# First two projection units on x without its inverse root, and a second transposition of x

## What is computed

```python
u = rmsnorm(x, norm_w)          # x * rsqrt(mean(x*x) + 1e-6) * norm_w, per token
proj = u @ w_in                 # 2048 x 20528
ml_i, ml_f, dn_b, dn_a = ...    # 48 small gate columns of proj
qkv = silu(causal_conv(proj[:, dn_qkv], width 4))   # 3 x 2048 columns
q, k = l2norm(heads(q)), l2norm(heads(k))
...
```

## Time and profile before

| | |
|---|---|
| time, median of 3 runs | 1907.54 us (1907.08 to 1909.92) |
| profiled execution | 1906.96 us, of which its span is 1905.2 us |
| PE busy | 1885.3 us (99%) |
| DVE busy | 1407.6 us (74%) |
| ACT busy | 911.0 us (48%) |
| DMA | 393.17 MB, 206 GB/s over the span |
| chain that ended last | PE 92%, DVE 4%, POOL 1%, ACT 1% |

### The profile page before, as it was taken

How to read it: one execution, slowest core, us unless ns; L and a number is a source line. 1 busy time by engine, 2 the same in 40 slices (tenths; PEclk the granted TensorE clock), 3 DMA queues, 4 the chain that set the end, 5 groups by cost and what they waited for, 6 DMA issues and landing times.

```text
span 1905.2 us, 27734 instructions
## 1 busy us (share of the span) xinstructions
PE 1885.3 (99%) x10964; PEld 1635.8 (86%) x10964; DVE 1407.6 (74%) x2068; ACT 911.0 (48%) x1394; POOL 328.5 (17%) x550
## 2 busy tenths in 40 slices
PE   8999999999999999999999999999999999999998
PEld 8999999878888989888888888888888888888886
DVE  5786877767989788889989667666464676657675
ACT  6546455445433433434445465554444455544544
POOL 1034425161212222313223100000000000111000
PEclk9999999999999999999999999999999999999999
DMA  8555454546788787777888857655656543544563
GB/s 263 149 159 177 124 176 144 155 155 194 263 271 288 255 270 238 238 261 248 288 293 307 297 188 233 232 177 186 196 169 203 175 133 126 185 147 150 186 224 132
DMA packets 209745, 393.17 MB, mean 206 GB/s; under 512 B 13000, under 2 KB 62448, under 8 KB 208208
## 3 DMA queue, kind: packets, MB, share of 16 engines
q1 hardware_dynamic: 191248, 323.17, 52.0%
q0 software_dynamic: 18224, 68.17, 11.2%
q10 hardware_dynamic: 144, 0.07, 0.0%
HBM read 387.13 MB, written 4.23 MB: 205 GB/s over the span
## 4 chain that ended last, share of the span: by engine, by line
PE 92%; DVE 4%; POOL 1%; ACT 1%; issue 1%; DMA 0%; SPq 0%; DVEq 0%; ACTq 0%; POOLq 0%
PE GB L2188 50%; PE GB L2215 19%; PE GB L2200 9%; PE GB L2203 5%; PE SB L419 1%; PE SB L1759 1%; DVE WL L2112 1%; PE SB L1751 1%; POOL TB L1122 1%; POOL XB L1125 1%; PE SB L1858 1%; PE SB L1865 1%; PE SB L829 1%; PE SB L1216 1%; ACT WH L2107 0%
## 5 line engine op out<-in xcount | busy, mean ns | idle before, releaser
L2112 DVE TENSOR_TENSOR WL<-raw,WH 128x1024 fp32r<-128x1024 f32 x605 | 730.9, 1235 | 180.3 <-ACT WH L2107 179.1
L2107 ACT ACTIVATE WH<-raw 128x1024 fp32r<-128x1024 f32 x605 | 622.7, 1059 | 312.2 <-PE GB L2188 226.2
L2188 PE MATMUL GB<-WH,uHL 128*128 128x512 f32 x1792 | 484.6, 392 | 1.2 <-DVE WL L2112 1.2
L2188 PEld LDWEIGHTS GB<-WH,uHL 128*128 128x128 f32 x1792 | 333.2, 188 | 69.2 <-issue 1.3
L2215 PE MATMUL GB<-uHL,WH 128*128 128x256 f32 x2048 | 291.4, 285 | 1.6 <-DVE uHL L455 1.6
L2188 PE MATMUL GB<-WH,hHL 128*128 128x512 f32 x1024 | 279.4, 395 | 0.0
L2188 PE MATMUL GB<-WL,uHL 128*128 128x512 f32 x896 | 276.1, 389 | 0.0
L2215 PEld LDWEIGHTS GB<-uHL,WH 128*128 128x128 f32 x2048 | 264.0, 192 | 2.9 <-DVE uHL L455 1.8
L2188 PEld LDWEIGHTS GB<-WH,hHL 128*128 128x128 f32 x1024 | 190.6, 188 | 41.1 <-issue 2.7
L1446 DVE SCALAR_TENSOR_TENSOR macc<-wm,csil,macc 128x512 f32<-128x512 f32 x300 | 209.5, 748 | 2.7 <-DMA wm<-in_w_mod 1.5
L2188 PEld LDWEIGHTS GB<-WL,uHL 128*128 128x128 f32 x896 | 168.2, 188 | 35.5
(11 more groups left out here) (408 smaller groups left out, 1911.9 us busy)
## 6 DMA issues: line engine op xcount, KB each, us to landing
raw<-in_w_in SPq DMA_DIRECT2D x512, 512.0 KB, 4.5
raw<-in_w_out SPq DMA_DIRECT2D x96, 512.0 KB, 5.2
wm<-in_w_mod POOLq DMA_DIRECT2D x64, 512.0 KB, 5.5
wm<-in_w_mod POOLq DMA_DIRECT2D x64, 256.0 KB, 4.3
xin<-in_x SPq DMA_DIRECT2D x4, 512.0 KB, 5.8
E<-decay_rows POOLq DMA_DIRECT2D x4, 512.0 KB, 4.2
hres<-in_x POOLq DMA_DIRECT2D x1, 2048.0 KB, 10.7
cin<-in_ctx POOLq DMA_DIRECT2D x1, 2048.0 KB, 11.5
```

Source lines behind the costliest of these rows:

```text
L2107: e.activation(place(s)[0][:, :, :], raw[s % NR][:, :, :], ACT.Copy).then_inc(*wh.inc("WH", s))
L2112: e.tensor_tensor(low[:, :, :], raw[s % NR][:, :, :], f32(high[:, :, :]), sub).then_inc(*wl.inc("WL", s))
L2188: m = e.matmul(banks[j][:, :], x[:, c, 128 * j:128 * j + 128], w[:, k, :], start=i == 0 and k == 0 and n == 0, stop=i == 7 and k == 1 and ...
```

## The change

x is loaded in eight parts of 256 columns, interleaved with the first five weight tiles, and `vcol` is loaded from ACT's queue. PE transposes the unscaled x as it lands; `uH` and `uL` are made from x times `norm_w` alone. Units 0 and 1 (`RAW = 2`) and the gates are computed on them. Slot 0 is computed by `first_pe` in another order (all of `uH` on `WH`, all of `uL` on `WH`, all of `uH` on `WL`). The sums of squares move to slots 2 to 5 and the inverse root to slots 5.5 and 6. The inverse root is spread over a row per token: DVE multiplies the identity by it, PE multiplies `ones` by the result between the two row groups of slot 7 (`norm_pe`), and ACT copies it to `rrow`. DVE multiplies the gates' result by `rrow` (in place of ACT's copy), and the results of units 0 and 1 too (`scaled_dve`, at slots 7 and 15, into `zz`, from which the convolutions then read). ACT scales x in place at slots 8 to 9.5, and x is transposed and split a second time (stage "u2", pairs 0 to 7 at slots 10, 11, 12, 13, 13.5, 14, 14.5 and 15.5), with `uH` of a pair overwritten once the slot of unit 1 that reads it is done. Slot s of unit 2 waits for pair s-16 of the second pass. 8 instead of 30 matmuls of `ones` run at the start.

```diff
+RAW = 2
...
+NXA, NXD, NXP = (2, 3, 4, 5, 6, 7, 8, 8.5, 9, 9.5), (5.5, 6), (6.5,)
...
     steps("u", -1, 2, 100)
     steps("u", 0, 6)
+    at("nxa", 0, NXA)
+    at("nxd", 0, NXD)
+    at("nxp", 0, NXP)
+    at("u2", 0, (10, 11, 12, 13, 13.5, 14, 14.5, 15.5))
     at("gates", 0, GATES)
     steps("cond", 60, 2)
...
-        nx_act = steps("nx_act", "warm", "s0", "s1", "s2", "s3", "sqrt", "x1a", "x1b", "x1c")
-        nx_dve = steps("nx_dve", "ss", "var", "inv", "w2", "wv", "rstd", "x0a", "x0b", "x0c")
+        nx_act = steps("nx_act", "warm", "s0", "s1", "s2", "s3", "sqrt", "row", "x0", "x1", "x2", "x3")
+        nx_dve = steps("nx_dve", "ss", "var", "inv", "w2", "wv", "rstd", "diag")
+        nx_pe = steps("nx_pe", "row")
+        z_dve = steps("z_dve", "z")
...
+        TU, TU2, THB, THA, TCTX, THX, TOA, TOB = 0, 8, 16, 24, 32, 40, 48, 52
...
+        def turn_act(e, base, H, pairs, scale, shift, *free, freed=None):
             for k in range(pairs):
                 if k == 0:
                     for said in free:
                         e.wait_ge(*said)
+                if freed:
+                    e.wait_ge(*freed(k))
...
-            claim(e, bank, 0, g_act.at("c"))
+            claim(e, bank, 0, g_dve.at("c"))
...
-            e.wait_ge(*g_pe.at("g"))
-            e.activation(rw[:, SS, :], SB[0][:, 0:256], ACT.Copy).then_inc(*g_act.inc("c"))
...
-            e.wait_ge(*g_act.at("c"))
+            e.wait_ge(*g_pe.at("g"))
+            e.wait_ge(*nx_act.at("row"))
+            e.tensor_tensor(r(SS), SB[0][:, 0:256], rrow[:, :], mul).then_inc(*g_dve.inc("c"))
+            e.wait_ge(*g_dve.at("c"))
...
         def norm_act(e):
-            e.wait_ge(*init.at("eps"))
-            e.activation(st[:, 62:63], eps[:, 0:1], ACT.Sqrt).then_inc(*nx_act.inc("warm"))
-            for i in range(2):
-                for j in range(2):
-                    n = 2 * i + j
-                    e.wait_ge(x_in[n], 16)
+            for j in range(2):
+                for i in range(2):
+                    n = 2 * j + i
+                    for p in range(4):
+                        e.wait_ge(x_in[4 * j + p], 16)
                     if n >= 2:
                         e.wait_ge(*nx_act.at(f"s{n - 2}"))
-                    e.activation(s_junk[:, 1024 * j:1024 * j + 1024], xin[:, i, 1024 * j:1024 * j + 1024], ACT.Square,
-                                 accum_out=st[:, n:n + 1]).then_inc(*nx_act.inc(f"s{n}"))
+                    e.activation(s_junk[:, 1024 * i:1024 * i + 1024], xin[:, i, 1024 * j:1024 * j + 1024], ACT.Square,
+                                 accum_out=st[:, 2 * i + j:2 * i + j + 1]).then_inc(*nx_act.inc(f"s{n}"))
+                    yield
             e.wait_ge(*nx_dve.at("var"))
             e.activation(st[:, 4:6], rs[:, 0:2], ACT.Sqrt).then_inc(*nx_act.inc("sqrt"))
-
-        XPARTS = {"a": slice(0, 512), "b": slice(512, 1024), "c": slice(1024, 2048)}
-
-        def scaled_act(e, c):
-            e.activation(xin[:, 1, XPARTS[c]], xin[:, 1, XPARTS[c]], ACT.Copy, scale=st[:, 5:6]).then_inc(*nx_act.inc("x1" + c))
-
-        def scaled_dve(e, c):
-            e.tensor_scalar(xin[:, 0, XPARTS[c]], xin[:, 0, XPARTS[c]], st[:, 4:5], None, mul).then_inc(*nx_dve.inc("x0" + c))
-
-        def busy_pe(e):
-
-            for said, n in ((init.at("ones"), 15), ((x_in[2], 16), 5), ((x_in[3], 16), 6), (nx_dve.at("ss"), 4)):
-                e.wait_ge(*said)
-                for _ in range(n):
-                    e.matmul(SB[3][:, 0:128], ones[:, :], ones[:, :], start=True, stop=True, skip_group_check=True)
+            yield
+            e.wait_ge(*nx_pe.at("row"))
+            e.activation(rrow[:, :], SB[2][:, 0:256], ACT.Copy).then_inc(*nx_act.inc("row"))
+            yield
+            e.wait_ge(*tr_pe.at("t", TU + 7))
+            for j in range(2):
+                for i in range(2):
+                    c = slice(1024 * j, 1024 * j + 1024)
+                    e.activation(xin[:, i, c], xin[:, i, c], ACT.Copy, scale=st[:, 4 + i:5 + i]).then_inc(*nx_act.inc(f"x{2 * j + i}"))
+                    yield
 
         def norm_dve(e):
             e.wait_ge(*nx_act.at("s3"))
             e.tensor_tensor(st[:, 4:6], st[:, 0:4:2], st[:, 1:4:2], add).then_inc(*nx_dve.inc("ss"))
             e.wait_ge(*nx_dve.at("ss"))
             e.tensor_scalar(rs[:, 0:2], st[:, 4:6], 1.0 / D, 1e-6, mul, add).then_inc(*nx_dve.inc("var"))
+            yield
             newton_dve(e, nx_dve, st[:, 4:6], rs[:, 0:2], rs[:, 2:4], nx_act.at("sqrt"))
             e.wait_ge(*nx_dve.at("rstd"))
+            for i in range(2):
+                v = e.tensor_scalar(junk[:, 128 * i:128 * i + 128], ident[:, :], st[:, 4 + i:5 + i], None, mul)
+            v.then_inc(*nx_dve.inc("diag"))
+            yield
+
+        def norm_pe(e, bank):
+            e.wait_ge(*nx_dve.at("diag"))
+            claim(e, bank, 2, nx_act.at("row"))
+            m = e.matmul(SB[2][:, 0:256], ones[:, :], junk[:, 0:256], start=True, stop=True, skip_group_check=True)
+            m.then_inc(*nx_pe.inc("row"))
+            yield
+
+        def busy_pe(e):
+
+            e.wait_ge(*init.at("ones"))
+            for _ in range(8):
+                e.matmul(SB[3][:, 0:128], ones[:, :], ones[:, :], start=True, stop=True, skip_group_check=True)
 
...
-            e.wait_ge(*slot.at("mm", end("qkv", r)))
+            e.wait_ge(*(z_dve.at("z", r) if r < RAW else slot.at("mm", end("qkv", r))))
...
             for j in range(4):
-                a = e.activation(y[:, j, :], half(banks[j // 2], j % 2), ACT.Identity,
+                a = e.activation(y[:, j, :], zz[:, j, :] if r < RAW else half(banks[j // 2], j % 2), ACT.Identity,
...
+        def scaled_dve(e, r, banks):
+            e.wait_ge(*slot.at("mm", end("qkv", r)))
+            e.wait_ge(*nx_act.at("row"))
+            for j in range(4):
+                v = e.tensor_tensor(zz[:, j, :], half(banks[j // 2], j % 2), rrow[:, :], mul)
+            v.then_inc(*z_dve.inc("z", r))
...
-                    e.scalar_tensor_tensor(out=y[:, j, sh:], in0=half(banks[j // 2], j % 2)[:, 0:256 - sh],
+                    e.scalar_tensor_tensor(out=y[:, j, sh:], in0=(zz[:, j, :] if r < RAW else half(banks[j // 2], j % 2))[:, 0:256 - sh],
...
                     e.wait_ge(*mark)
             if (unit.kind, unit.n) == ("qkv", 0) or (i == 0 and (unit.kind, unit.n) in (
                     ("yb", 0), ("ya", 0), ("kaC", 0), ("kaX", 0))) or ((unit.kind, unit.n) == ("out", 0) and i in (0, 4)):
-                e.wait_ge(*arrived(unit.kind, unit.n, i))
-            e.wait_ge(*wl.at("WL", s))
+                if s:
+                    e.wait_ge(*arrived(unit.kind, unit.n, i))
+            if (unit.kind, unit.n) == ("qkv", RAW):
+                e.wait_ge(*tr_dve.at("l", TU2 + i))
+            if s:
+                e.wait_ge(*wl.at("WL", s))
             if unit.mode == "two":
                 m = halves_pe(e, unit, s, banks)
             elif unit.mode == "tok":
                 m = tokens_pe(e, unit, s, banks, (0,) if last_unit else (0, 1), stages)
             else:
-                m = channels_pe(e, unit, s, banks, stages)
+                m = channels_pe(e, unit, s, banks, stages) if s else first_pe(e, banks)
...
+
+        def first_pe(e, banks):
+            wh_, wl_ = place(0)
+            for said, x, w in ((tr_act.at("h", TU), uH, wh_), (tr_dve.at("l", TU), uL, wh_), (wl.at("WL", 0), uH, wl_)):
+                if w is wh_:
+                    e.wait_ge(*wh.at("WH", 0))
+                e.wait_ge(*said)
+                for k in range(2):
+                    for j in range(4):
+                        m = e.matmul(half(banks[j // 2], j % 2), w[:, k, 128 * j:128 * j + 128], x[:, k, :],
+                                     start=x is uH and w is wh_ and k == 0 and j % 2 == 0, stop=False, skip_group_check=True)
             return m
...
             banks = pair(u)
+            if k == "qkv" and n < RAW:
+                scaled_dve(e, n, banks)
...
+        FIRST_X = {0: (0,), 1: (1, 2), 2: (3,), 3: (4, 5), 4: (6, 7)}
         block = ctx.enter_context(nc.Block())
 
         @block.sync
         def _(e):
-            for i in range(2):
-                for j in range(2):
-                    e.dma_start(xin[:, i, 1024 * j:1024 * j + 1024],
-                                x_rows[:, i, 1024 * j:1024 * j + 1024]).then_inc(x_in[2 * i + j], 16)
-            e.dma_start(vcol[:, :], A["c_vcol"]).then_inc(vcol_in, 16)
             for s in range(NS):
+                for p in FIRST_X.get(s, ()):
+                    e.dma_start(xin[:, :, 256 * p:256 * p + 256],
+                                x_rows[:, :, 256 * p:256 * p + 256]).then_inc(x_in[p], 16)
...
             e.dma_start(ident[:, :], A["c_ident"]).then_inc(ident_in, 16)
-            norm_act(e)
-            split_act(e, 0)
-            e.wait_ge(*nx_dve.at("rstd"))
-            scaled_act(e, "a")
-            scaled_act(e, "b")
```

(48 more changed lines are left out.)

## The result

| | before | changed |
|---|---|---|
| median of 4 runs | 1908.03 us | 1920.77 us (1920.13 to 1921.32) |
| ratio | 1 | 1.0065 (1.0048 to 1.0083) |
| profiled execution | 1906.96 us | 1920.51 us |
| its span | 1905.2 us | 1918.7 us |

A forecast was written before the change was run, and what follows sets the result against it. PE's list of work behind the first product was taken to bound the kernel. -6.5 (start) + 1.4 + 0.4 (root) + 3.5 (pairs) + 8.0 (L797) = +6.8 us gave 1914.0 us, range 1905.0 to 1917.5.

The forecast's parts named there:

- the later tiles fall out of the sum: At the start: tiles behind tile 2 bring in 0.5 to 1 MB each per 3.31 us, less than the rate allows.
- the price of the long wait: PE's wait at the sum of squares behind slot 16: put into the sum as 8.0 us.
- Bound, and direction: Behind the first product PE's list of work decides; the change was forecast slower, by 6.8 us in the sum.
- First product near 8.2, slot 1 near 12.6: Start of the kernel on PE: first product at 8.2 us, slot 1 at 12.6, range 11.8 to 13.5.
- The price of 5.8 us: Slot 0 wholly at half pace, by the clock gate's rule taken in full: 5.8 us, slot 1 starting at 14.5.
- T: Start of slot 6 on PE: 35.66 us before, forecast 29.15, a gain of 6.5 (5.6 to 7.3).
- The root's wait of 1.4 us: In the middle of slot 7 PE waits 1.4 us for the root's row matmul; bounds 0.3 and 2.5.
- DVE's chain to T+49.1: DVE's steps from slot 10 to the end of slot 15, ending with `uL` of pair 7 at T+49.1.
- The wait of 8.0: Behind slot 16 PE's sum of squares (L797) claims `SB3` and waits 8.0 us for pair 7; bounds 5 and 10.
- The sum: Whole kernel: -6.5 (start) + 1.4 + 0.4 (root) + 3.5 (pairs) + 8.0 (L797) = +6.8 us.
- Behind slot 17 nothing gives it back: PE's later waits, 4.3 us in all, hang on DVE work that shifts too; at most 1 us comes back.

The follow-up runs named there:

- the filled wait: The changed kernel with 30 matmuls of ones that nobody reads put into PE's wait ahead of the sum of squares: 1917.45 us, ratio 1.005.
- pair 7 late: The changed kernel with pair 7 of the second transposition at slot 17.5 instead of 15.5, behind the sum of squares: 1913.97 us, ratio 1.0033.
- the wait in the kernel before: The kernel before with one wait added on PE ahead of the sum of squares, for the convolution's third tap: 1917.8 us, ratio 1.0052.
- the spread kernel: The changed kernel with GpSimd's loads behind tile 4 instead of 2 and the second transposition spread over slots 11 to 18.5: 1909.94 us, ratio 1.0007.

## Why the prediction was wrong, point by point

Two steps failed. The first is that "the later tiles fall out of the sum": with GpSimd's loads beside them they cost 2.8 us. The second is the price of the long wait: it was put into the sum at its length alone, and the half clock behind it, 4.4 us, at nothing.

- **Bound, and direction: right.** PE's list of work decides, and the change adds to it more than it takes away.
- **First product near 8.2, slot 1 near 12.6: right** (8.12 and 12.88). The slow pace was in the range taken from the earlier trace rows. It was partly luck: 12.6 lies between two cases, and each kernel's profiled execution shows one of them. With the filled wait slot 0 ran at the full clock and slot 1 started at 11.89, in the changed kernel slot 0 lasted 12.53 - 8.12 = 4.4 us. By the rule of the Trainium skill (page "TensorE: Matmul & The Clock Gate", "Part 1: The HAM clock gate") the array is slow by default and fast only after sustained activity; the trace of the changed kernel agrees for most of slot 0, at a granted clock of 0.50 up to about 11.4 us. The price of 5.8 us worked out from that rule was too high, since the clock rises in the course of slot 0.
- **"The later tiles fall out of the sum": wrong, 2.8 us.** T came to 31.93, not 29.15. The term left out was GpSimd's 1 MB, which starts behind tile 2 and so moved forward with it from 14.18 to 12.3, where it took 31.8% of the DMA engines. With it out of the way T is 29.27.
- **The root's wait of 1.4 us**: 1.05. Right in place.
- **DVE's chain to T+49.1: right**, T+48.3, step by step. **The wait of 8.0**: 6.06, plus 1.02 at the gates' small transposes (L508), which claim `SB1` behind pair 1. That claim was overlooked, but it only moves part of the same wait forward.
- **What is behind the wait: wrong, 4.4 us.** I priced the idle time of PE as its length. The clock falls in it, and 1.70 us more for the sum of squares, 2.31 more for slot 17 (5.26 against 2.95) and 0.38 more for slot 18 follow. The Trainium skill's rule had been weighed for the start only, though it speaks of any idle PE; it should have been put to the 8 us wait of my own sum. The filled wait and the one in the kernel before show it from both sides.
- **The sum**: 6.8 forecast, plus 2.8 (tiles), plus 4.0 (clock, up to slot 18), less 0.7 (the sum of squares starts at T+48.4, not T+49.1) is 12.9. Measured at the start of slot 18 it is 12.7: 89.03 against 76.31, where slots 17 and 18 start at 73.36 and 76.31 in the trace of before. The 0.2 between them is a slip of the forecast, which has PE at the sum of squares at T+41.3 in its total and at T+41.1 in the wait. Behind it 0.38 us are the slow beginning of slot 18, and 0.4 a longer wait for `X` (1.6 us at L946 against 1.2 at L914), which makes the 13.5 of the two profiled executions. The forecast's last step has a slip too: 1913.8 and 0.6 are 1914.4, not 1914.0.
- **Behind slot 17 nothing gives it back: right.** The reverse was not foreseen: where the wait was taken away, 3 to 4 us came back as later waits, since ACT and DVE stay behind up to the score products.

## What to carry to other kernels

An idle time of PE can cost the slow clock behind it besides its own length: ask it of each wait in a sum, and fill a wait that can't be removed with matmuls that nobody reads (30 of them gained 3.3 and 3.6 us here). A step moved earlier takes along what hangs on it: look for the queue that is started by the landing you move forward, and what it will compete with there. Before a bank or buffer gets one more user in a hand-made order, list who claims it next and when the new user's reader, on an engine that now has more to do, will be done.

## What the runs showed of the hardware

After an idle PE of 3.02 and 3.17 us (pair 7 late), 5.17 (the wait in the kernel before) and 6.06 (the changed kernel) the granted clock was at 0.50, and in the spread kernel it fell within a microsecond after a wait of 2.25. But the length alone doesn't decide: 2.07 us (slot 4 of the changed kernel) and 2.91 (slot 4 with the filled wait) left it at 1.00, and the wait of 1.56 us ahead of slot 0 was followed by 0.50 in one execution of the kernel before with its added wait and by 1.00 in the one without. In the changed kernel the clock fell 2 us into the idle time (74.30 to about 76.3), in the kernel before with the added wait 4 us into it (72.96 to 77.0). PE then worked for 9.5 and 9.0 us (the sum of squares, all of slot 17 and the beginning of slot 18) before the clock was at 1.00 again; after the 3.02 us it was back in 6.1, after the 3.17 in 5.6, after the 2.25 in 4.2. What decides between these was not tried. In the first microseconds the clock column says 1.00 while the matmuls run at the slow pace; there the distance of their starts is the better witness.
